# State-space heads of a Trainium2 kernel taken in pairs: products on alternating column halves, running sums spread from alternating rows

## What is computed

```python
N_SSD_HEADS, HEAD_DIM, SSD_CHUNK, SSD_STATE = 16, 64, 128, 128   # 512 tokens: 4 chunks

dt = softplus(dt_raw + dt_bias)                  # per token and head
a_cs = cumsum(-exp(a_log) * dt)                  # running sum inside each chunk
decay = exp(where(causal, a_cs[l] - a_cs[s], -inf))
y_diag = einsum("bclgn,bcsgn->bcgls", c, b) * decay @ (x * dt)   # inside a chunk
y_off  = exp(a_cs) * c @ state_carried_in                        # from chunks before
y = y_diag + y_off + d_skip * x
y = rms_norm_per_group(y * silu(z)) * norm_w
```

## Time and profile before

| | |
|---|---|
| median of three runs | 2591.09 us |
| profiled execution | 2591.52 us |
| its span | 2589.7 us |
| PE busy | 2439.7 us (94%) |
| DVE, ACT, POOL busy | 44%, 36%, 40% |
| the state-space stage, first running sum to last product | 1674.7 to 1785.0 us of the span |
| two heads in its steady part | 13.15 us |

### The profile page before, as it was taken

How to read it: one execution, slowest core, us unless ns; L and a number is a source line. 1 busy time by engine, 2 the same in 40 slices (tenths; PEclk the granted TensorE clock), 3 DMA queues, 4 the chain that set the end, 5 groups by cost and what they waited for, 6 DMA issues and landing times.

```text
span 2589.7 us, 28909 instructions
## 1 busy us (share of the span) xinstructions
PE 2439.7 (94%) x10584; PEld 1857.8 (72%) x10610; DVE 1129.2 (44%) x1439; ACT 930.9 (36%) x1352; POOL 1041.0 (40%) x479
## 2 busy tenths in 40 slices
PE   7979799999999989799999978899999999899999
PEld 5767578888887767588888867666645557688887
DVE  5876664222436965752223358345135552211100
ACT  4235633333132245433332143233215553333321
POOL 4659134444436665244444424211420012244442
PEclk9989899999999999899999979999988889799999
DMA  4211122333732211123336613111310001232332
GB/s 146 81 49 57 49 73 90 97 97 112 246 112 90 66 49 58 49 82 97 97 97 189 200 49 98 57 33 34 98 49 9 16 17 57 60 95 96 97 97 89
DMA packets 59873, 216.06 MB, mean 83 GB/s; under 512 B 6656, under 2 KB 6912, under 8 KB 59792
## 3 DMA queue, kind: packets, MB, share of 16 engines
q1 hardware_dynamic: 52272, 187.62, 23.4%
q10 hardware_dynamic: 7520, 27.33, 3.2%
HBM read 212.83 MB, written 2.10 MB: 83 GB/s over the span
## 4 chain that ended last, share of the span: by engine, by line
PE 83%; DVE 11%; ACT 3%; issue 2%; DMA 0%; DVEq 0%; SPq 0%; ACTq 0%
PE bank L1146 23%; PE bank L1148 22%; PE bank L1147 22%; PE bank L1556 2%; PE bank L1586 2%; DVE xc L957 2%; PE bank L1569 2%; DVE bank L717 1%; ACT prob L430 1%; PE bank L1159 1%; PE bank L1297 1%; PE bank L1503 1%; PE bank L1488 1%; PE bank L1272 1%; DVE root L676 1%
## 5 line engine op out<-in xcount | busy, mean ns | idle before, releaser
L282 POOL TENSOR_TENSOR wl<-raw,wh 128x1024 fp32r<-128x1024 f32 x351 | 860.4, 2452 | 1521.6 <-ACT wh L351 1521.1
L1146 PE MATMUL bank<-hh,wh 128*128 128x512 f32 x2024 | 817.6, 404 | 57.9 <-DVE conv L719 22.2
L1147 PE MATMUL bank<-hl,wh 128*128 128x512 f32 x2024 | 799.0, 395 | 0.0
L1148 PE MATMUL bank<-hh,wl 128*128 128x512 f32 x2024 | 798.7, 395 | 0.0
L351 ACT ACTIVATE wh<-raw 128x1024 fp32r<-128x1024 f32 x351 | 369.2, 1052 | 676.0 <-PE bank L1148 657.8
L1146 PEld LDWEIGHTS bank<-hh,wh 128*128 128x128 f32 x2024 | 386.3, 191 | 176.5 <-issue 38.1
L1148 PEld LDWEIGHTS bank<-hh,wl 128*128 128x128 f32 x2024 | 386.4, 191 | 82.7
L1147 PEld LDWEIGHTS bank<-hl,wh 128*128 128x128 f32 x2024 | 387.3, 191 | 81.0 <-issue 4.3
L1146 PE MATMUL bank<-ah,wh 128*128 (+1 forms) x528 | 208.0, 394 | 0.0
L1148 PE MATMUL bank<-ah,wl 128*128 (+1 forms) x528 | 207.0, 392 | 0.0
L1147 PE MATMUL bank<-al,wh 128*128 (+1 forms) x528 | 204.9, 388 | 0.0
(11 more groups left out here) (297 smaller groups left out, 2713.8 us busy)
## 6 DMA issues: line engine op xcount, KB each, us to landing
raw<-stream SPq DMA_DIRECT2D x351, 512.0 KB, 3.6
ada_w<-ada ACTq DMA_DIRECT2D x48, 512.0 KB, 4.6
x<-x_t ACTq DMA_DIRECT2D x4, 512.0 KB, 7.8
out_t<-x SPq DMA_DIRECT2D x8, 256.0 KB, 2.1
cst<-consts SPq DMA_DIRECT2D x1, 640.0 KB, 11.1
tmp<-masks SPq DMA_DIRECT2D x1, 320.0 KB, 11.2
par<-params SPq DMA_DIRECT2D x1, 253.0 KB, 4.4
cst<-consts SPq DMA_DIRECT2D x1, 224.0 KB, 8.0
```

The source lines that it names most:

```text
L282: nc.gpsimd.tensor_tensor(wl[:, slot, :], raw[:, raw_slot, :], wh[:, slot, :].bitcast(F32), ALU.subtract).then_inc(lo_ready, 1)
L1146: mm(dst, wh[:, slot, w], xh, start=start, stop=False)
L1147: mm(dst, wh[:, slot, w], xl, start=False, stop=False)
L1148: return mm(dst, wl[:, slot, w], xh, start=False, stop=stop)
```

## The change

Heads are taken two at a time, pair t being heads 2t and 2t + 1.

- **Products.** In each chunk the product of the even head and that of the odd head now follow each other, so that weights go to the lower 64 columns of the array and then to the upper 64, and so on. All 8 products inside the chunks come first, then the 6 with the carried state. The count is the same: 14 matmuls per pair. Instead of `decayed` they wait for `within_ready`, and between the two groups for `across_ready`.
- **Running sums.** The weights and biases for dt are laid out twice in the host's arrangement, at columns 0 to 15 and 64 to 79, so `dt_t` and `acs_t` become 128 rows high and hold the heads twice. `running(t)` spreads the even head from rows 0 to 15 and the odd one from rows 64 to 79, into banks 0 and 1. The few DVE and ACT instructions that make dt now go over 128 partitions and no longer over 16. It is issued between the two halves of a value tile.
- **Buffers.** The factor inside the chunk has two buffers per parity of the pair: `tmp[2]`, `tmp[3]` for even pairs and the tables `cos`, `sin`, no longer needed by then, for odd pairs. The factor for the carried state stays in `tmp[4]`, `tmp[5]`.
- **Order on ACT and DVE.** ACT first takes the exponentials inside the chunk, then, after `y_ready` of the pair before, those for the carried state. DVE multiplies, finishes the pair before, and only then makes the differences of the next pair.

```diff
-            def running(h):
-                if h == 0:
+            head_rows = [slice(0, NH), slice(HD, HD + NH)]
+
+            def running(t):
+                if t == 0:
                     pe.wait_ge(lin_free, MB + M_SQ)
-                if h >= 2:
-                    pe.wait_ge(run_diff, h - 1)
-                    pe.wait_ge(run_exp, 2 * h - 3)
-                mm(bank[:, h % 2, :], ident[0:NH, h:h + 1].to_broadcast([NH, P]), acs_t[:, :], start=True, stop=True).then_inc(run_ready, 1)
+                else:
+                    pe.wait_ge(run_diff, 2 * t)
+                    pe.wait_ge(run_exp, 2 * t)
+                for e, rows in enumerate(head_rows):
+                    at = rows.start + 2 * t + e
+                    last = mm(bank[:, e, :], ident[rows, at:at + 1].to_broadcast([NH, P]), acs_t[rows, :], start=True, stop=True)
+                last.then_inc(run_ready, 1)
...
+            halves_of = [slice(0, HD), slice(HD, P)]
             running(0)
-            for h in range(NH):
-                t, s, half = h // 2, h % 2, slice((h % 2) * HD, (h % 2) * HD + HD)
-                if h + 1 < NH:
-                    running(h + 1)
-                half_v(h)
-                if s == 0 and t:
+            for t in range(KT):
+                half_v(2 * t)
+                if t + 1 < KT:
+                    running(t + 1)
+                if t:
                     turn_v(t - 1)
-                pe.wait_ge(decayed, 2 * h + 2)
-                if h == 0:
+                half_v(2 * t + 1)
+                if t == 0:
                     pe.wait_ge(state_out, 3)
-                if t >= 2 and s == 0:
+                if t >= 2:
                     pe.wait_ge(y_out, t - 1)
+                pe.wait_ge(within_ready, 2 * t + 2)
                 for b in range(BLK):
                     at = slice(b * P, b * P + P)
-                    last = mm(bank[half, 2 + t % 2, at], xg[:, b, h * HD:h * HD + HD], tmp[:, 2 + s, at], start=True, stop=b == 0)
-                    if b:
-                        last = mm(bank[half, 2 + t % 2, at], carried[:, b - 1, h * HD:h * HD + HD], tmp[:, 4 + s, at], start=False, stop=True)
+                    for e, half in enumerate(halves_of):
+                        mm(bank[half, 2 + t % 2, at], xg[:, b, t * P + e * HD:t * P + e * HD + HD], within[t % 2][e][:, at],
+                           start=b == 0, stop=b == 0, skip_group_check=True)
+                pe.wait_ge(across_ready, 2 * t + 2)
+                for b in range(1, BLK):
+                    at = slice(b * P, b * P + P)
+                    for e, half in enumerate(halves_of):
+                        last = mm(bank[half, 2 + t % 2, at], carried[:, b - 1, t * P + e * HD:t * P + e * HD + HD], across[e][:, at],
+                                  start=False, stop=True, skip_group_check=True)
                 last.then_inc(y_ready, 1)
-                if s == 1 and t:
+                if t:
                     sum_y(t - 1)
```

More of the change, by code:

```diff
@@ L89, in build @@
         small = sb("small", [P, 3])
-        eps, q_gain, neg_a = small[:, 0:1], small[:, 1:2], small[0:NH, 2:3]
+        eps, q_gain, neg_a = small[:, 0:1], small[:, 1:2], small[:, 2:3]
         neg_sink = sb("neg_sink", [P, NH])
@@ L183, in build @@
         xs_turned, xg_ready, xd_ready, state_ready, state_out = (stage(n) for n in ("xs_turned", "xg_ready", "xd_ready", "state_ready", "state_out"))
-        run_ready, run_diff, run_exp, decayed, y_ready, y_out = (stage(n) for n in ("run_ready", "run_diff", "run_exp", "decayed", "y_ready", "y_out"))
+        run_ready, run_diff, run_exp, diff_exp = (stage(n) for n in ("run_ready", "run_diff", "run_exp", "diff_exp"))
+        within_ready, across_ready, y_ready, y_out = (stage(n) for n in ("within_ready", "across_ready", "y_ready", "y_out"))
         y_normed, ssdh_ready, ssdl_ready = (stage(n) for n in ("y_normed", "ssdh_ready", "ssdl_ready"))
@@ L243, in build @@
         v_tmp = [root, rstd]
+        within = [[tmp[:, 2, :], tmp[:, 3, :]], [cos, sin]]
+        across = [tmp[:, 4, :], tmp[:, 5, :]]
         SQUARES_AFTER = {0: [], 1: [], 2: [], 3: [0], 4: [1, 2], 5: [3, 4]}
@@ L530, in _ @@
             scaled_tiles(N1, 0)
-            af(neg_a[:, :], par_m("a_log", rows=NH), ACT.Exp).then_inc(neg_a_ready, 1)
+            af(neg_a[:, :], par_m("a_log"), ACT.Exp).then_inc(neg_a_ready, 1)
             for i in range(XT):
@@ L565, in put_v @@
                 af(v2[:, :, t * P:t * P + P], bank[:, 7, :].rearrange("p (a b) -> p a b", a=BLK), ACT.Copy).then_inc(v2_out, 1)
-            for h in range(NH):
-                s = h % 2
-                act.wait_ge(run_ready, h + 1)
-                if h >= 2:
[L571 to L578, removed]
+            for t in range(KT):
[8 more added lines that the diff above has]
+                if t:
+                    if t == 1:
                         act.wait_ge(state_out, 3)
-                    put_v(h // 2 - 1)
-                    act.wait_ge(y_out, h // 2)
-                    square(SB + S_SSD + h // 2 - 1, z[:, h // 2 - 1, :])
+                    put_v(t - 1)
+                    act.wait_ge(y_out, t)
+                    square(SB + S_SSD + t - 1, z[:, t - 1, :])
             copy_v(KT - 1)
@@ L962, in _ @@
             dve.wait_ge(used, CB + B_DT + 1)
-            ts(dt_t[:, :], bank[0:NH, (MB + M_DT) % 4, :], par_m("dt_bias", rows=NH), None, ALU.add).then_inc(lin_free, 1)
+            ts(dt_t[:, :], bank[:, (MB + M_DT) % 4, :], par_m("dt_bias"), None, ALU.add).then_inc(lin_free, 1)
             dve.wait_ge(dt_log, 1)
@@ L968, in _ @@
             link(ts(neg_a[:, :], neg_a[:, :], -1.0, None, ALU.mult))
-            link(ts(tmp[0:NH, 2, :], dt_t[:, :], neg_a[:, :], None, ALU.mult))
+            link(ts(tmp[:, 2, :], dt_t[:, :], neg_a[:, :], None, ALU.mult))
             for b in range(BLK):
-                last = nc.vector.tensor_tensor_scan(acs_t[:, b * P:b * P + P], ones[0:NH, :], tmp[0:NH, 2, b * P:b * P + P], 0.0, ALU.mult, ALU.add)
+                last = nc.vector.tensor_tensor_scan(acs_t[:, b * P:b * P + P], ones, tmp[:, 2, b * P:b * P + P], 0.0, ALU.mult, ALU.add)
             last.then_inc(dt_ready, 1)
@@ L1023, in _ @@
             dve.wait_ge(cb_out, 2)
-            for h in range(NH):
-                s, g = h % 2, h // 8
-                if h + 1 < NH:
[L1027 to L1033, removed]
+            for t in range(KT):
+                g = t // 4
+                for e in range(2):
+                    dve.wait_ge(diff_exp, 2 * t + e + 1)
+                    tt(within[t % 2][e], within[t % 2][e], cb[:, g, :], ALU.mult).then_inc(within_ready, 1)
+                for e in range(2):
+                    dve.wait_ge(run_exp, 2 * t + e + 1)
+                    tt(across[e], across[e], xc[:, 10 + g, :], ALU.mult).then_inc(across_ready, 1)
+                if t:
+                    finish_y(t - 1)
+                if t + 1 < KT:
+                    run_differences(t + 1)
             finish_y(KT - 1)
@@ L1405, in _ @@
                     pe.wait_ge(root_ready, RB + 1)
-                    for w, src in enumerate((dt_t, acs_t)):
+                    for w, src in enumerate((dt_t[0:NH, :], acs_t[0:NH, :])):
                         for b in range(BLK):
@@ L1513, in _ @@
                     pe.wait_ge(y_out, KT)
-                    pe.wait_ge(run_exp, 2 * NH)
+                    pe.wait_ge(run_exp, NH)
                     pe.wait_ge(lin_free, MB + M_SQ)
```

32 lines of the change are left out of this document (16 added, 16 removed).

## The result

The changed kernel takes **2548.84 us** (median of 4 runs, 2546.3 to 2551.62) against 2590.08 us before (4 runs, 2587.66 to 2596.64): ratio 0.984, 95% interval 0.981 to 0.986. The forecast was 2567.5, range 2560 to 2575.

The account below looks back on a forecast made before the run. PE's own stream was taken as the bound; products 11.7, spreads 7.35, waits 1.4, entries 1.0 and start 2.2 summed to 23.6 us saved, giving 2567.5 us from the median, range 2560 to 2575.

Parts of the forecast that it names:

- The bound: Whole kernel: PE holds 83% of the chain; a change pays only by shortening PE's stream or its waits.
- rival 4: State-space pairs: ACT's wait for `y_ready` blocks the turn's copies, ACT and DVE set the loop; 2579 us, chance 0.03.
- Products, 11.7 us: State-space pairs: products on alternating column halves overlap in full, 28 passes taking 1.67 us; saves 7 x 1.67 = 11.7 us.
- The rule on weight loads: State-space products: loads overlap matmuls in flight only across row groups, so column halves would gain nothing; the prediction doubted it.
- Rival 2: State-space products do not overlap at 128 columns because of weight loads; 12.3 us back, 2580 us, chance 0.05.
- rival 3: State-space products: each change of column half drains the array, 33 us lost against 23.6; 2600 us, chance 0.03.
- Spreads, 7.35: State-space running sums: two spreads on different row groups overlap, thirteen become six; saves 7 x 1.05 = 7.35 us.
- Waits and entries, 2.4: Steady state-space pairs: PE's waits for DVE go, 1.4 us, and fewer changes of matmul shape save 1.0 us.
- The start, 2.2: Start of the state-space stage: shorter stop, 3.3 us idle, and pair 0 ending near 1693.1 against 1695.28; saves 2.2 us.
- what the trace loses comes off the median nearly one to one: Whole kernel: the profiled execution was 1.8 us above its span and 0.4 us from the median.
- Rival 5: Clock at the state-space start: not lowered, 2563 us, or low longer, 2572.5 us; counted within the forecast's 0.80.
- the 0.02 for something not seen: No place named: chance 0.02 for an outcome the prediction does not see, half of it no gain.

Follow-up runs that it names:

- b_again: The kernel before, unchanged, run again for a second profile; its profiled execution took 2576.16 us.
- a_halves_apart: The changed kernel with all products of the even head before those of the odd head, in both groups; a pair took 10.37 us instead of 9.88.
- a_spread_later: The changed kernel with the spread of pair 1 issued behind the second half of the first value tile, for the first pair alone; median 2547.57 us.

## Why the prediction was wrong

*The bound.* Right. PE's stream sets the time, and nothing else in the stage became a bound: PE is busy 9.88 of 9.88 us in a pair, so rival 4 is out.

*Products, 11.7 us.* Right in size and cause. The earlier trace rows carried over to 128 columns and column halves: 28 passes in 1.67 us. The rule on weight loads cited from the Trainium skill, "TensorE: Matmul & The Clock Gate", Part 3, does not hold for column halves: with 28 different loads nothing stands between the passes. Rival 2 is out, and so is rival 3, changes of the half that drain the array.

*Spreads, 7.35.* Right: 1.05 for two, 1.91 without different rows.

*Waits and entries, 2.4.* Right and slightly short. From the end of the first pair to that of the eighth, 89.7 us became 67.15: 22.5, against 11.7 + 7.35 + 1.4 + 1.0 = 21.4.

*The start, 2.2.* 4.5 measured. The stop was not shorter (3.87, not 3.3), since the first two spreads overlap as well and PE reaches the stop sooner; I had overlooked this. PE resumed 7.95 us after the first spread, where 8.1 were forecast. Then pair 0 ended 8.1 us later and not 10.2 (1.9 + 5.1 + 3.2), since only 5.2 of them lay at half clock: that is nearly all of the 2.3 too much. The length of this low stretch differs between executions of one kernel (3.4 and 10.2 in two traces of before, 6.8 in both of the changed kernel), so these 2.3 us can't be told from chance.

*What failed* is a term that the sum puts at nothing without a reason: that what follows the stage keeps its time. All terms of the sum lie in the stage, and the attention heads behind it have none. They gave 17.0 us in the trace. (The sentence that what the trace loses comes off the median nearly one to one held: 45.0 and 41.2.) The heads have two ways to run, 163.5 us or up to 180.5, at the same code. The trace of before had shown the slow one: ten low stretches, 13.65 us apart, in a stage that I read no stretch of. Its chain and its waits don't point to them, only the clock row of its page does. By their times most executions of before run so, which puts it in the median, and none of ten of the changed kernel. The forecast left 17 us out, and these are nearly the 18.7 by which it missed. In the traces, what is left of the 21.4 between 45.0 and 23.6 is 2.3 at the start and 1.1 in the steady part, both above, and 2.3 gained ahead of the stage less 1.1 lost behind it, mostly clock as well: the low stretches ahead of the stage add up to 133 us before and 130 after, those between it and the heads to 37.5 and 41.0. Rival 5 had the clock as a mechanism, but in the wrong place and with under a third of the size (4.6 to 5 us): I gave it the first stop of the stage only. What came falls to the 0.02 for something not seen. It was luck, good luck for the change, that the heads of before mostly run the long way: from the trace of b_again (2576.16) the same sum would have given about 2552, and the change 27 to 30 us.

What is shown: that the 17 us are the low clock in the heads (same work to 0.01 us beside it), that they come and go between executions of one kernel, and that 0.44 us of work ahead of the heads turns them on in the changed kernel and 0.88 us turns them off in the kernel before. What is not: what lets the clock fall in the heads, and why the changed stage leads to a start at which it mostly doesn't. Nothing in the runs says that a change of this kind would do so again; of the 41 us about 25 belong to the change (24 by the estimate at full clock, and 24.4 between the fastest executions of both kernels, 2542.3 and 2566.7), and some 16 to the clock, nearly all of it in the heads.

## What to carry to other kernels

Small float32 products that write different halves of the PSUM partitions, or read different row groups, can be put next to each other, and here each pair cost what one costs; look in the trace of the same kernel for a place that does it already, and take its start-to-start price. Before forecasting a total, ask for the granted clock of every later stage, and not of the changed one alone: a repeating stage in which low stretches come at the distance of one iteration is in step with the clock, and a shift of less than a microsecond ahead of it can end that, or start it. Such a kernel needs ten executions or more, read one by one before a median is taken, and span times mean granted clock beside them: it separated the change (24 us) from the clock where four executions gave 41.

## What the runs showed of the hardware that was not expected

- Matmuls on one column half pass earlier ones on the other half: in a_halves_apart L1506 starts at 1707.35, ahead of L1500 up to 1707.67, within one block. The Trainium skill, "TensorE: Matmul & The Clock Gate", Part 3, calls matmuls strictly first in, first out; by these rows that holds within a half at most.
- Two spreads of 16 rows, from rows 0 and 64 on, run at once (1.05 us against 1.91 from the same rows).
- The same program runs its 16 heads in 163.6 or in 180.5 us (b_again and before), and 0.44 us of work ahead of them took the changed kernel from 163.5 to 180.4.
- A stop of 1.16 us (a_spread_later) was followed by as long a low stretch (6.8 us) as came with one of 3.87. That the stop is its cause is not shown.
